# Attention scores for two heads side by side on TensorE, and top-k selection of two token tiles per pass, in a one-core encoder step

## What is computed

```python
logits = jnp.einsum('bqhd,bsd->bqsh', qi_b, ki)
score = jnp.einsum('bqsh,bqh->bqs', jax.nn.relu(logits), wi_b).astype(jnp.float32)
_, idx = lax.top_k(score, top_k)
s = jnp.einsum('bqhgd,bqkhd->bqhgk', q_b, k_sel).astype(jnp.float32) * (HEAD_DIM ** -0.5)
p = jax.nn.softmax(s, axis=-1).astype(v.dtype)
return jnp.einsum('bqhgk,bqkhd->bqhgd', p, v_sel)
```

## Time and profile before

| | us |
|---|---|
| median of three runs | 2713.3 (2709.68 to 2714.39) |
| the profiled execution, its own time | 2712.45 |
| its span, first to last instruction | 2710.5 |
| TensorE busy | 2553.4 (94%) |
| VectorE busy | 995.9 (37%) |
| ScalarE busy | 944.0 (35%) |
| GpSimd busy | 1362.5 (50%) |
| TensorE matmul records of scores (L902), first and last start | 1275.3 to 2058.5 |

### The profile page before, as it was taken

One profiled execution on the slowest core, in us unless ns is written; L12 is line 12 of the kernel. 1 busy time (PEld: TensorE's weight loads), 2 busy tenths in 40 slices (PEclk: granted clock), 3 DMA queues, 4 the chain that ended last, 5 costly groups with the idle time before them and its releaser, 6 DMA issues.

```text
span 2710.5 us, 40319 instructions
## 1 busy us (share of the span) xinstructions
PE 2553.4 (94%) x16301; PEld 2270.4 (84%) x16301; DVE 995.9 (37%) x1941; ACT 944.0 (35%) x1608; POOL 1362.5 (50%) x833
## 2 busy tenths in 40 slices
PE   8999998987999998897989899999999898999997
PEld 7888888776999998894489888888657888999997
DVE  1000006046710006038463588888654636000004
ACT  4333333323233232227434343333353333333230
POOL 3777565442666655341052567666302516666562
PEclk9999999998999999897799999999798999999999
DMA  4444432433233322333122223333401212433331
GB/s 139 121 119 114 154 94 67 107 99 129 86 94 90 90 71 64 104 86 113 56 63 62 64 76 103 110 94 95 150 1 59 59 39 63 128 115 94 94 92 59
DMA packets 420110, 245.07 MB, mean 90 GB/s; under 512 B 22817, under 2 KB 410977, under 8 KB 418657
## 3 DMA queue, kind: packets, MB, share of 16 engines
q1 hardware_dynamic: 389088, 195.65, 25.5%
q10 hardware_dynamic: 26480, 23.21, 2.8%
q0 software_dynamic: 4368, 23.73, 2.4%
HBM read 218.79 MB, written 21.74 MB: 89 GB/s over the span
## 4 chain that ended last, share of the span: by engine, by line
PE 75%; DVE 10%; DVEq 6%; issue 3%; ACT 2%; DMA 1%; POOL 1%; ACTq 1%; POOLq 0%; SPq 0%
PE LIN L645 63%; DVEq L1426 5%; DVE M L1423 5%; PE LIN L902 3%; PE TR L915 2%; PE TR L929 2%; DVE Y L1519 1%; PE LIN L722 1%; PE TR L698 1%; DMA spill_cl<-YCL 1%; DVE Y L1514 1%; PE LIN L884 1%; POOL WL L1754 1%; DVEq L1422 1%; PE TR L846 0%
## 5 line engine op out<-in xcount | busy, mean ns | idle before, releaser
L1754 POOL TENSOR_TENSOR WL<-WRAW,WH 128x1024 fp32r<-128x1024 f32 (+1 forms) x378 | 886.8, 2349 | 497.6 <-ACT WH L972 490.9
L645 PE MATMUL LIN<-XH,WH 128*128 128x256 f32 (+4 forms) x3016 | 834.5, 321 | 55.2 <-DVE Y L1462 25.3
L645 PE MATMUL LIN<-XH,WL 128*128 128x256 f32 (+4 forms) x3016 | 826.3, 318 | 0.0
L645 PE MATMUL LIN<-XL,WH 128*128 128x256 f32 (+4 forms) x3016 | 825.1, 318 | 0.0
L645 PEld LDWEIGHTS LIN<-XH,WH 128*128 128x128 f32 (+1 forms) x3016 | 530.5, 191 | 95.7 <-issue 50.5
L645 PEld LDWEIGHTS LIN<-XL,WH 128*128 128x128 f32 (+1 forms) x3016 | 531.1, 191 | 35.2
L645 PEld LDWEIGHTS LIN<-XH,WL 128*128 128x128 f32 (+1 forms) x3016 | 528.3, 191 | 34.8
L645 PE MATMUL LIN<-HH,WH 128*128 128x256 f32 (+2 forms) x1632 | 465.3, 307 | 8.5 <-POOL HL L1826 6.8
L645 PE MATMUL LIN<-HL,WH 128*128 128x256 f32 (+2 forms) x1632 | 462.9, 306 | 0.0
L645 PE MATMUL LIN<-HH,WL 128*128 128x256 f32 (+2 forms) x1632 | 462.2, 305 | 0.0
L972 ACT ACTIVATE WH<-WRAW 128x1024 fp32r<-128x1024 f32 (+2 forms) x382 | 393.0, 1030 | 145.3 <-PE LIN L645 54.8
(11 more groups left out here) (191 smaller groups left out, 2165.2 us busy)
## 6 DMA issues: line engine op xcount, KB each, us to landing
WRAW<-in_ffn_gate SPq DMA_DIRECT2D x88, 512.0 KB, 3.8
WRAW<-in_ffn_up SPq DMA_DIRECT2D x88, 512.0 KB, 3.8
WRAW<-in_ffn_down SPq DMA_DIRECT2D x64, 512.0 KB, 3.9
WRAW<-in_w_mix_in SPq DMA_DIRECT2D x44, 512.0 KB, 3.8
WRAW<-in_ffn_down SPq DMA_DIRECT2D x32, 384.0 KB, 3.4
WRAW<-in_w_mix_out SPq DMA_DIRECT2D x16, 512.0 KB, 3.9
WRAW<-in_w_mem_q SPq DMA_DIRECT2D x16, 512.0 KB, 3.9
WRAW<-in_w_mem_o SPq DMA_DIRECT2D x16, 512.0 KB, 3.9
```

What stands on the lines that cost most here:

```text
L645: last = pe.matmul(LIN[0:pr.rows, pr.slot, out:out + w], wt[:, pr.tile % RING, c, 0:pr.rows], x[:, c, col:col + w], start=(c == 0 and wt i ...
L1754: pool.tensor_tensor(WL[:, n % RING, 0:nk, 0:width], WRAW[:, n % 2, 0:nk, 0:width], WH[:, n % RING, 0:nk, 0:width].bitcast(F32), ALU.subtr ...
```

## The change

Two edits that have nothing to do with each other.

1. Scores are issued for two jobs at once, one head on partitions 0 to 63 and one on 64 to 127, their products alternating. For that the order of heads becomes 0, 1, 2, 3 instead of 0, 2, 1, 3 (so odd and even alternate). The pair now waits until both halves of `LIN` have been read, that is until the second peak of the pair before; and it is issued before every second turn instead of one job's before every turn.
2. `select` handles two tiles in one loop: max, max, drain, replace, replace, drain. `M8` gets a row of eight for each.

```diff
-            for kvg in range(2) for hh in (0, 2, 1, 3)]
+            for kvg in range(2) for hh in range(4)]
...
-        M8 = place("M8", [P, 8], F32, region(32))
+        M8 = place("M8", [P, 2, 8], F32, region(64))
...
-                    def scores(a):
-                        t, col, rows, keys, kvg, hh = jobs[a]
-                        h, lo = 4 * kvg + hh, 64 * (hh % 2)
-                        if a >= 2:
-                            pe.wait_ge(nm_ready, s0 + a - 1)
-                        same = (kvg == 0) == (lo == 0)
-                        kmat = (KSA if same else KSB) if rows == DEC else (KPA if same else KPB)
+                    def scores(p):
+
+                        t, col, rows, keys, kvg, hh = jobs[2 * p]
+                        if p:
+                            pe.wait_ge(nm_ready, s0 + 2 * p)
                         for k0 in range(0, keys, 512):
                             w = min(512, keys - k0)
-                            last = pe.matmul(LIN[0:rows, a % 2, k0:k0 + w],
-                                             (QA1 if g.sample else QA0)[lo:lo + 64, h // 2, col:col + rows],
-                                             kmat[lo:lo + 64, k0:k0 + w], start=True, stop=True)
-                        last.then_inc(s_done, 1)
+                            for odd in range(2):
+                                h, lo = 4 * kvg + hh + odd, 64 * odd
+                                same = (kvg == 0) == (lo == 0)
+                                kmat = (KSA if same else KSB) if rows == DEC else (KPA if same else KPB)
+                                mm = pe.matmul(LIN[0:rows, odd, k0:k0 + w],
+                                               (QA1 if g.sample else QA0)[lo:lo + 64, h // 2, col:col + rows],
+                                               kmat[lo:lo + 64, k0:k0 + w], start=True, stop=True)
+                                if k0 + w == keys:
+                                    mm.then_inc(s_done, 1)
...
                     scores(0)
-                    scores(1)
                     for a in range(len(jobs)):
-                        if a + 2 < len(jobs):
-                            scores(a + 2)
+                        if a % 2 == 0 and a + 2 < len(jobs):
+                            scores(a // 2 + 1)
                         if a % 4 == 0 and a:
                             values(a // 4 - 1)
                         turn(a)
...
             def select(g):
-                for t, rows, keys, rounds in score_tiles(g):
-                    at_ = SCORE_AT[(g.index, t)]
-                    sc = SC[0:rows, at_:at_ + keys]
-                    with dve.Fori(0, rounds):
-                        dve.max(M8[0:rows, :], sc)
+                tiles = score_tiles(g)
+                for k in range(0, len(tiles), 2):
+                    pair = tiles[k:k + 2]
+                    keys_of = [SC[0:rows, SCORE_AT[(g.index, t)]:SCORE_AT[(g.index, t)] + keys] for t, rows, keys, _ in pair]
+                    with dve.Fori(0, pair[0][3]):
+                        for i, sc in enumerate(keys_of):
+                            dve.max(M8[0:pair[i][1], i, :], sc)
                         dve.drain()
-                        dve.match_replace(sc, M8[0:rows, :], sc, TAKEN)
+                        for i, sc in enumerate(keys_of):
+                            dve.match_replace(sc, M8[0:pair[i][1], i, :], sc, TAKEN)
                         dve.drain()
-                    dve.tensor_scalar(sc, sc, CUT, FAR, ALU.is_gt, ALU.mult)
+                    for sc in keys_of:
+                        dve.tensor_scalar(sc, sc, CUT, FAR, ALU.is_gt, ALU.mult)
```

## The result

The changed kernel takes 2691.46 us (median of four runs, 2690.05 to 2693.93), the kernel before 2713.72 us beside it: ratio 0.9922, 95% interval 0.9905 to 0.9939. The forecast was 2693. Measured once more on another chip it took 2691.96 us, ratio 0.9915 (0.9901 to 0.9928). The total came out, partly by luck; two of the sum's terms did not, and they are what the experiments are about.

The account below looks back on a forecast made before the run. TensorE, busy for 94% of the 2710.5 us span, was taken as the bound. Terms of -0.2, -12.6, -19.5, +1.5, +5.4 and +5 gave -20.4 us, so 2692.1, forecast as 2693 us, range 2684 to 2703 (55%).

Parts of the forecast that it names:

- Selection: Two tiles in one loop save VectorE about 40 us; at the barrier before att 1 only 0.2 us comes off.
- Two heads at once: Paired scores in att 0 and att 1 overlap: a pair takes one job's time plus 0.15 us.
- The new wait: Attention: paired scores wait for the previous pair's second peak; plain rounds gain 1.3, 0, 2.3, 0.3 and 0.4 us.
- Late exponents: After rounds with values, ScalarE's exponent stands behind a later copy, delaying scaling: 0.3 us for 18 rounds, 5.4 us lost.
- The clock of att 0: The clock rises at the same distance from the start, so the last tile's first 10 us run at 0.50: +5 us.
- rival 1: In both attention segments the clock comes up sooner, since paired scores fill the array: 2676 us, chance 13%.
- The sum: Whole kernel: -0.2 - 12.6 - 19.5 + 1.5 + 5.4 + 5 = -20.4 us.
- Rival 2: At 512 to 1024 keys TensorE's idle time keeps the clock low, some 19 us: 2712 us, chance 7%.
- Rivals 3 and 4: Paired scores: 3, half an overlap, 2705 us, 12%; 4, no overlap and a longer loop, 2732 us, 13%.
- the table: Round times in att 0 and att 1 by keys and clock, before and new; segment gains 12.6 and 19.5 us.

Follow-up runs that it names:

- Run 1: Only the selection of two tiles a pass, with scores and order of heads as in the kernel before: 2712.11 us, ratio 0.9992 to the kernel before.
- run 3: The changed kernel with heads in the order 0, 2, 1, 3, so both heads of a pair lie on the same 64 partitions: 2736.99 us, ratio 1.0078.
- Run 7: The changed kernel with 72 unread products of 128 columns on TensorE ahead of each attention segment: 2690.13 us, ratio 0.9908.
- run 4: The changed kernel with one head's products ahead of the other's over 512 keys, instead of alternating: 2690.74 us, ratio 0.9916.

## Why the prediction was right, step by step

- **Selection, 0.2 us.** Right. Run 1 has the interval 0.9983 to 1.0001, and GpSimd ends last at the barrier. VectorE spends 29 us less waiting ahead of `max` and 11 us less in `max` and `match_replace`, the forecast 40, and it changes nothing. The chain on the page of before runs through selection (`DVEq L1426 5%; DVE M L1423 5%`), a tenth of the span, and the chain after the change doesn't: VectorE was last at the barrier by 0.3 us, and that is all that a chain through it was worth.
- **Two heads at once, one job plus 0.15 us.** The mechanism is right, and run 3 shows what it is worth. The size was a little high: a pair costs 0.0 to 0.1 us more than one job (1.97 for 1.91 at 1024 keys, 1.13 for 1.05 at 512). Over 36 pairs that is some 3 us better than the sum had it.
- **The new wait.** Right: the chain alternates between TensorE and VectorE once a round, and plain rounds came at 5.24 us (forecast 5.49) at 1024 keys and 3.12 (1323.51 to 1326.63; forecast 3.30) at 512.
- **Late exponents, 0.3 us for each of 18 rounds: wrong in mechanism and size.** No exponent set such a round. In att 0 the scaling stood behind `out_lo`, which waits for the values just issued; 0.7 to 0.9 us of idle TensorE a round, 5.7 in seven. In att 1 the second turn waits for the copy of the first in six rounds, 1.0 to 1.2 us each, and in the round of 640 keys for `out_lo`, 0.9 us: 7.4. That makes 13 us instead of 5.4. Both were hidden before but in the first such round of att 0, where the sentence "without a step on another engine" was already untrue: a turn followed every job's scores, so VectorE had 0.76 to 1.04 us to spare ahead of a peak and ScalarE a job's scores for its copy. I named what stood behind the new wait on TensorE, and not what stood in the queues of VectorE and ScalarE.
- **The clock of att 0, +5 us.** Wrong sign. It rose 17 us earlier than at the same distance from the start, and in att 1 13 us earlier: rival 1 came partly true. Its reason, that paired scores fill the array as values do, has run 3 for it, where pairs on one half leave the rise at 49 and 28.6 us. From the segments, what is left for the clock after the corrections above is about -1 us in att 0 (-9.0 + 12.6 + 1.5 - 5.7, with 1.5 for the pairs) and -2 in att 1 (-14.3 + 19.5 + 2 - 1.5 - 7.4); these are remainders, not measurements. Run 7 says that low clock at the very start of att 1 is nearly free.
- **The sum.** 8 us too little for lost cover stand against 3 for the pairs, and about 6 in att 0 and 2 in att 1 for the clock. The two segments alone are 23.3 us shorter (25.5 in the repeated run), more than the 20.2 they were to give, and the 5.5 (4.3) us that the stretches outside them grew by at the lower clock, which the sum didn't have, brought the total back. That it came within 2 us is partly luck.
- **Rival 2.** It didn't come: the clock stood at 1.00 from 13.7 to 109.2 us of att 1, and in att 0 for the tile of 512 keys up to the last 6.3 us. Its trace is that fall: the last values took 3.71 us (3.46 before).
- **Rivals 3 and 4.** Half an overlap: refuted by the timeline above, where both heads' first records start ahead of any second one, and by run 4. There the four records of one head stand ahead of the other's in the program, and a pair still takes what one head takes, 2.0 us at 1024 keys. The Trainium skill, "TensorE: Matmul & The Clock Gate", Part 3, says that matmuls start and end in strict program order. By that a pair would have taken about 1.75 of a job's time there (an estimate: three of the first head's four records stand ahead of it); across the two halves of the array the trace of run 4 doesn't agree. No overlap: run 3 makes it and ends at +23 us; the changed kernel doesn't behave so. What "TensorEngine Tiling (Array Packing)", Key Properties, in the Trainium skill says of tiles that work in parallel holds here for fp32 products split by rows.

## What to carry to other kernels

When two jobs of an engine are paired, go through the queue of every other engine and ask for each instruction what it waits for and what now stands right behind it: the slack of one job that hid it is gone, and here that took back 13 of the 32 us of the table. Work that waits for the latest result (a store, a low part, a copy of a finished sum) belongs one job later in the queue than the work that feeds the next product. A busy share that falls by 49 us while the span falls by 18 says that such waits exist, and the chain of waits behind the round with the extra product names them. The old trace can name them too: look for the round with the shortest cover.

## What the runs showed of the hardware

- Two fp32 products on row halves 0 to 63 and 64 to 127 run fully side by side (1.97 us for a pair of 1024 keys, 1.91 for one), and don't have to alternate in the program: run 4 gives the same time with one head's products first. On the same half the pair of 896 keys takes 3.20 us instead of 1.77.
- The granted clock rose from 0.50 to 1.00 earlier when pairs filled both halves of the array: 32 instead of 49 us into att 0, 8.5 and 13.7 (two runs) instead of 26.5 us into att 1. With pairs on the same half it rose after 49 and 28.6 us. Once `out_lo` had moved, it rose 15 us into att 0. Filling the wait ahead of a segment kept it at 1.00 for the first 1.7 us of att 0 and the first 7 of att 1.
- Where TensorE is busy nearly all the time, the lower clock costs about half a microsecond for each one: the 4708 records after att 1 took 645.9 us with 31.5 us at 0.50, and 650.2 with 39.2.
